# Expert table: one of the eight tokens of a slice weighed on GpSimd, two on VectorE, five on ScalarE

## The reference, cut to what matters

```python
top_s, top_i = lax.top_k(sc, PEER_TOPK)
...
best_s, best_pos = lax.top_k(cand_s, PEER_TOPK)
idx = jnp.take_along_axis(cand_i, best_pos, axis=-1)
gate = jax.nn.softmax(best_s, axis=-1)
...
    uc = u[ic]
    act = jnp.einsum("cd,ced->ce", xc, uc).astype(jnp.float32)
    hid = (jax.nn.gelu(act, approximate=False) * gc).astype(xc.dtype)
    return jnp.einsum("ce,ced->cd", hid, v[ic])
```

## Time and profile before

| | us |
|---|---|
| median of 3 runs | 2331.58 |
| lowest and highest | 2330.25, 2332.45 |
| the profiled execution | 2331.98 |
| its span, first to last instruction | 2330.2 |
| its mean granted TensorE clock | 0.975 of full speed |
| VectorE busy in it | 1529.7 (66%) |
| ScalarE busy | 863.7 (37%) |
| GpSimd busy | 435.6 (19%) |

### The profile page before, as it was taken

One profiled execution on the slowest core, in us unless ns is written; L12 is line 12 of the kernel. 1 busy time (PEld: TensorE's weight loads), 2 busy tenths in 40 slices (PEclk: granted clock), 3 DMA queues, 4 the chain that ended last, 5 costly groups with the idle time before them and its releaser, 6 DMA issues. The chain is left out here.

```text
span 2330.2 us, 29399 instructions
## 1 busy us (share of the span) xinstructions
PE 2198.9 (94%) x11221; PEld 1904.0 (82%) x11221; DVE 1529.7 (66%) x2699; ACT 863.7 (37%) x1431; POOL 435.6 (19%) x308
## 2 busy tenths in 40 slices
PE   7999899899999899889999999999998999988998
PEld 6777788688999889888788888999996798877677
DVE  4545434425999989955888888688887534335634
ACT  3345323222333645863333333333334332222322
POOL 0100000000122010001433425266661000023200
PEclk9999999999999999999999999999998999989999
DMA  5321133202678674778999999799992322210220
GB/s 215 107 86 55 51 140 141 90 33 65 233 251 254 184 245 148 207 217 304 371 381 387 383 381 368 250 358 365 357 329 112 109 91 91 98 47 1 109 100 36
DMA packets 211836, 451.32 MB, mean 194 GB/s; under 512 B 13808, under 2 KB 133616, under 8 KB 204912
## 3 DMA queue, kind: packets, MB, share of 16 engines
q1 hardware_dynamic: 174832, 315.21, 39.6%
q0 software_dynamic: 36864, 134.23, 15.9%
HBM read 404.56 MB, written 44.83 MB: 193 GB/s over the span
## 5 line engine op out<-in xcount | busy, mean ns | idle before, releaser
L1603 PE MATMUL bank<-Vh,Hh 128*128 128x512 f32 x768 | 300.1, 391 | 4.6 <-DVE Hl L1686 4.5
L1605 PE MATMUL bank<-Vh,Hl 128*128 128x512 f32 x768 | 300.2, 391 | 0.0
L1604 PE MATMUL bank<-Vl,Hh 128*128 128x512 f32 x768 | 300.1, 391 | 0.0
L1625 ACT ACTIVATE Vh<-Vr 128x1024 fp32r<-128x1024 f32 x128 | 135.9, 1061 | 301.8 <-PE bank L1605 296.5
L933 PE MATMUL bank<-XH,Ue 128*128 128x384 f32 x672 | 232.9, 347 | 14.8 <-DVE Ue L922 14.8
L971 POOL DMA_INDIRECT ring<-in_v,gidx x128 | 204.7, 1599 | 165.4 <-DVE x_res L983 71.5
L934 PE MATMUL bank<-XL,Ue 128*128 128x384 f32 x672 | 227.8, 339 | 0.0
L935 PE MATMUL bank<-XH,Ue 128*128 128x384 f32 x672 | 227.5, 339 | 0.0
L1681 DVE TENSOR_TENSOR Vl<-Vr,Vh 128x1024 fp32r<-128x1024 f32 x128 | 156.3, 1221 | 49.1 <-ACT Vh L1625 46.2
L971 POOL DMA_INDIRECT ring<-in_u_rows,gidx x92 | 114.9, 1248 | 380.1 <-DVE ghid L976 204.2
L1603 PEld LDWEIGHTS bank<-Vh,Hh 128*128 128x128 f32 x768 | 144.6, 188 | 35.4 <-DVE Hl L1686 6.3
(11 more groups left out here) (380 smaller groups left out, 4935.2 us busy)
## 6 DMA issues: line engine op xcount, KB each, us to landing
Vr<-in_v SPq DMA_DIRECT2D x128, 512.0 KB
ur<-in_u SPq DMA_DIRECT2D x86, 512.0 KB
W<-in_w_stream SPq DMA_DIRECT2D x19, 2048.0 KB, 8.4
Gr<-gates SPq DMA_DIRECT2D x32, 768.0 KB
XT<-in_u SPq DMA_DIRECT2D x42, 512.0 KB
early<-ar SPq DMA_DIRECT2D x84, 192.0 KB
A<-early SPq DMA_DIRECT2D x84, 192.0 KB
xs<-in_w_mixer SPq DMA_DIRECT2D x14, 1024.0 KB
```

Of the source, the lines that this page charges most:

```text
L1603: pe.matmul(ps, Hh[r][:, tok], Vh[r][:, cut], start=p == 0, stop=False)
L1604: pe.matmul(ps, Hh[r][:, tok], Vl[r][:, cut], start=False, stop=False)
L1605: mm = pe.matmul(ps, Hl[r][:, tok], Vh[r][:, cut], start=False, stop=p == PK - 1)
L1625: act.activation(Vh[q % RV][:], Vr[q % RR][:], ACT.Copy).then_inc(v_hi, 1)
```

## The change

ScalarE keeps tokens 0 to 4, VectorE weighs tokens 5 and 6 (256 instead of 384 columns), GpSimd weighs token 7 by a `tensor_scalar` with the gate as a scalar per partition, for which it waits for the two one-hot tiles of the slice. TensorE waits for a third semaphore, `weighed_p`. GpSimd's list is split: fetches 0 to 27, the 16 weighings of the first tile, fetches 28 to 35, the 32 weighings of the second and third.

```diff
-    ON_ACT = 5
+    ON_ACT, ON_DVE = 5, 2
...
         @block.gpsimd
         def _(pool):
             pool.memset(ones, 1).then_inc(onesd, 1)
             pool.wait_ge(gat.ready, 1)
-            for s in range(DOTS_TABLE):
+
+            def weigh(tt):
+                for j in range(tt * NSL, (tt + 1) * NSL):
+                    pool.wait_ge(hot_made, 2 * j + 2)
+                    for k in range(ON_ACT + ON_DVE, S):
+                        one = hot[0][j % 2][:, k]
+                        last = pool.tensor_scalar(one, one, ijg[:, 2, j * S + k:j * S + k + 1], None, ALU.mult)
+                    last.then_inc(weighed_p, 1)
+
+            first = DOTS[0] + DOTS[1] + DOTS[2] + RG - 1
+            for s in range(first):
                 gat.fetch(pool, s)
+            weigh(0)
+            for s in range(first, DOTS_TABLE):
+                gat.fetch(pool, s)
+            weigh(1)
+            weigh(2)
...
                     pe.wait_ge(weighed_a, j + 1)
                     pe.wait_ge(weighed_d, j + 1)
+                    pe.wait_ge(weighed_p, j + 1)
...
-                    some = hot[0][r][:, ON_ACT:]
-                    dve.tensor_tensor(some, some, bc(ijg[:, 2, tok + ON_ACT:tok + S], P), ALU.mult).then_inc(weighed_d, 1)
+                    some = hot[0][r][:, ON_ACT:ON_ACT + ON_DVE]
+                    dve.tensor_tensor(some, some, bc(ijg[:, 2, tok + ON_ACT:tok + ON_ACT + ON_DVE], P), ALU.mult).then_inc(weighed_d, 1)
```

More of the change, by code:

```diff
@@ L1108, in phase_table @@
         first = ctx.enter_context(nc.sbuf_tensor("stage", [P, PK * Q_TOK], F32))
-        gexp, gdiff, chosen, t3, t3o, hot_made, weighed_a, weighed_d, built, copied, onesd = signals(
-            nc, ctx, "g_exp g_diff chosen t3_turned t3_out hot_made weighed_a weighed_d built copied t_ones")
+        gexp, gdiff, chosen, t3, t3o, hot_made, weighed_a, weighed_d, weighed_p, built, copied, onesd = signals(
+            nc, ctx, "g_exp g_diff chosen t3_turned t3_out hot_made weighed_a weighed_d weighed_p built copied t_ones")
         block = ctx.enter_context(nc.Block())
```

## The result

| | median us | lowest to highest | runs |
|---|---|---|---|
| before | 2330.42 | 2326.94 to 2335.5 | 20 |
| changed | 2334.24 | 2330.44 to 2338.84 | 20 |

The ratio is 1.0016, with a 95% interval of 1.001 to 1.0022: the change costs 3.8 us. That is less than the 0.2% that I had set as the bound, and yet the interval leaves out zero. I had said 2332.0, with 0 to 0.6 us added. So the time lies in the range, but the forecast's own reason (nothing on the path) leaves some 3 us unexplained, and those are what the experiments are about.

What follows compares the result with a forecast made beforehand. The table's 13.55 us four-slice round, a chain of waits through VectorE, ScalarE and TensorE, was taken as the bound. From 2331.98 us, 0 taken from the path and 0 to 0.6 added gave 2332, own range 2330 to 2336, overall 2328 to 2347.

Steps and rivals of the forecast that it cites:

- The round adds up without VectorE's weighing: Expert table: four slices take 13.55 us through comparisons, ScalarE, TensorE and low half; VectorE's weighing is on no step.
- 0.13 us a slice saved: VectorE's weighing, 128 fewer columns: 0.13 us a slice, 6.3 us in all, none of it on the path.
- The moved fetches, the third condition, 0 to 0.6 us: GpSimd's later fetches cost nothing; TensorE's one more condition per slice adds 0 to 0.6 us in all.
- Cost of the operation, d = 0.4 and x = 0.22: GpSimd's 128-column operation takes d, 0.4 us, and holds VectorE up by x, 0.22 us a slice, within idle time.
- x = d − 0.18: VectorE's delay x from a GpSimd operation lasting d: 0.18 us less than d, taken from a 1.08 us wait.
- The dear operation: Slower rival: GpSimd's operation takes 0.8 us, giving 2345, or 1.26, giving +35 and 2367; chance 0.12.
- They take turns: SBUF reads: GpSimd waits for VectorE's current two-input product, then VectorE's next waits for GpSimd; one turn every slice.
- the good row at 2146.21: Earlier trace: GpSimd's 512-column product took 2.19 us, beginning 0.16 us after VectorE's product; turns held.
- the bad one at 2153.77: Earlier trace: GpSimd's product lasted 5.31 us instead of 1.90 behind three undelayed VectorE products, beginning 0.07 before the first.
- The rival of starved turns: Slower rival: GpSimd, passed over, follows the next slice's comparisons; 15.5 a round, +23 us, 2355; chance 0.13 (2337 to 2357).
- a first half: First two slices of a four-slice round: comparisons 2.40, ScalarE 1.62, TensorE 2.09, sum 6.11 us; 7.76 if starved.
- One slice in five, 2337: Mild form of the starved-turns rival: if GpSimd is passed over in one slice in five, the time is 2337 us.

Runs made afterwards that it cites:

- e1: Kernel before with VectorE weighing two tokens and nobody weighing the eighth: 2331.93 us, ratio 1.0001 to the kernel before.
- e6: Kernel before with each slice's two comparisons swapped, ScalarE waiting only for the weighed tile: 2321.37 us, ratio 0.9965 to the kernel before.
- e3: Kernel before plus an unneeded 128-column GpSimd fill per slice, TensorE waiting for it, fetches split: 2329.3 us, ratio 0.9994 to the kernel before.
- e8: The change plus a 128-column fill of a spare tile on VectorE behind its weighing: 2336.71 us, ratio 1.0025 to the kernel before.
- e10: As e7, but VectorE's weighing waits for its tile alone and TensorE for both: 2313.56 us, ratio 0.9931 to the kernel before.
- e7: The change with comparisons swapped, ScalarE and GpSimd waiting only for the weighed tile: 2317.58 us, again 2316.78, ratios 0.995 and 0.9939 to the kernel before.

## Why the prediction was nearly right, and where it was wrong

The time came to lie in the range, but not for the reason given: turns were missed in a quarter of the slices, and that this cost 3.8 us and not more was luck, since the missed turn was short and seven of the twelve bad slices stand where no comparison waits for them.

*The round adds up without VectorE's weighing:* right, shown by e1 (no gain from an operation that is simply gone) and by the good rounds of 13.53. In e6, where the waits are gone, the same weighing counts in full.
*0.13 us a slice saved:* right, 558 to 425 ns.
*The moved fetches, the third condition, 0 to 0.6 us:* right, shown by e3.
*Cost of the operation, d = 0.4 and x = 0.22:* the operation's own time is 0.48 where it gets its turn behind the product that it waits for (in the good slice it ends at 782.30, the weighing ended at 781.82), and 0.39 where it had been passed over (in the bad one the comparison that went ahead ended at 795.27 + 1.22 = 796.49, GpSimd at 796.88). I was at most 0.08 short. The comparison behind it was held less than I said, 2.43 instead of 2.35: x = 0.08, and 0.11 at the most (1327 against 1218 ns). By x = d − 0.18 it would have been 0.30. The dear operation, a rival, did not come.
*They take turns:* **this is the step that failed.** I took the good row at 2146.21 of the earlier trace rows as the rule and the bad one at 2153.77 as an accident, priced as a rival. In 12 of 48 slices the turn is missed. The mean that I had given for GpSimd, 0.6 to 0.9, was 1.10 ((36 × 0.84 + 12 × 1.89) / 48). "TensorE waiting for ScalarE, never for GpSimd" is wrong in those seven places, where the records still name ScalarE, and by 0.2 us in an eighth, the first slice of the second tile.
*The rival of starved turns* was the right mechanism at the wrong size. I let the turn come after both comparisons of the next slice, 2.87 + 0.4 after the tiles, for 7.76 − 6.11 = 1.65 us in a first half and 2.0 in a round. It comes after one, 1.89 + 0.06 after the tiles, and with TensorE's start 0.26 behind it costs 0.55. "One slice in five, 2337" should have been one in four at a third of that price, with seven of the twelve off the path: 5 × 0.55 = 2.8 us. What I said separates good from bad (whether GpSimd begins before or after VectorE's product) was wrong: in both kinds it begins 0.06 after. The question was whether the product behind it is ready.

The Trainium skill, "SBUF — State Buffer", section "Who interferes with whom", has the two engines exclude each other for a whole instruction, whoever comes first. The runs agree that GpSimd waits for all of VectorE's product. They differ in two ways: VectorE's comparison was held 0.08 us by an operation of 0.39 to 0.48, and GpSimd, first to wait, still loses to VectorE's next product if that is ready.

**Open:** how the choice between the two engines is made; the rule above describes the slices of these traces and no more. It doesn't explain the 5.31 us row, which was passed over more than once. That TensorE starts 0.26 us after GpSimd's recorded end (0.15 in the first slice) but 0.06 after ScalarE's is measured, its cause was not tried. Some 1 us of the change's 3.8 is not assigned to a slice.

## What to carry to other kernels

Find the pace in a repeating round, by what ends last at each wait, before asking which engine is busiest: taking work from an engine whose waits then grow gives nothing, and here cost 3.8 us. A helper on GpSimd that reads SBUF beside VectorE's two-input products needs slack for one more whole product than its own turn, and each of its instructions needs that anew. First let the longest branch start on the one operand that it needs: reordering two comparisons was worth 8 us in time and 0.94 us in every round, and only behind it did the same share on GpSimd shorten the round (12.59 to 12.26) and the earlier weighing once more (to 12.02 to 12.15).

## What the runs showed of the hardware that I had not expected

- A waiting GpSimd operation is passed over by a VectorE product that is already free to go (0.84 against 1.89 us; in e8 0.84 against 1.97 beside equal neighbours; in e10 1.76 against 1.51 in all slices), and had its turn behind it. Whether the next two-input product is ready sorts all 288 slices of six traces.
- VectorE is held far less than the operation lasts: 0.08 us in the change, 0.05 in e7, for 0.48 us on GpSimd. Whether the comparison behind the weighing starts 0.02 us before the weighing's end or 0.08 behind it, it ends 1.31 behind it (13 slices of the change, 1327 to 1227 ns long).
- A fill on GpSimd, which only writes, took 0.205 us each of 48 times and waited for none of VectorE's products.
- TensorE's start follows GpSimd's recorded end by 0.26 us (0.15 in the table's first slice), and ScalarE's by 0.06.
